# Two up projections by seven half-size products for eight, with the weight sums shared by GpSimd and VectorE

## The reference, cut to what matters

```python
hn = rmsnorm(h, ffn_norm[i])                                   # (512, 1024)
h = h + jnp.square(jax.nn.relu(hn @ ffn_w1[i])) @ ffn_w2[i]    # 1024 -> 4096 -> 1024
gate = jax.nn.sigmoid(rmsnorm(h, ple_norm[i]) @ ple_w_gate[i])
```

## Time and profile before

| | us |
|---|---|
| median of 3 runs | 2130.05 |
| lowest and highest | 2128.93, 2130.39 |
| span of the profiled execution | 2127.2 |
| PE busy in it | 2098.9 |
| DVE, ACT, POOL busy in it | 1014.4, 805.4, 936.1 |

### The profile page before, as it was taken

One profiled execution on the slowest core, in us unless ns is written; L12 is line 12 of the kernel. 1 busy time (PEld: TensorE's weight loads), 2 busy tenths in 40 slices (PEclk: granted clock), 3 DMA queues, 4 the chain that ended last, 5 costly groups with the idle time before them and its releaser, 6 DMA issues.

```text
span 2127.2 us, 26516 instructions
## 1 busy us (share of the span) xinstructions
PE 2098.9 (99%) x9908; PEld 1705.7 (80%) x9908; DVE 1014.4 (48%) x1580; ACT 805.4 (38%) x1243; POOL 936.1 (44%) x436
## 2 busy tenths in 40 slices
PE   9999999999999999999999999999999999999998
PEld 7777888888888866888888887878867888888887
DVE  7996623122356555532132355572454466254463
ACT  7766322122343157322222355352244343232232
POOL 5984544444444410444444442444443444444442
PEclk9999999999999999999999999999999999999999
DMA  5332432222222222232222221222211222322221
GB/s 193 133 115 79 145 113 82 96 100 97 99 81 99 100 90 90 80 117 81 100 97 99 99 91 49 104 82 98 98 60 60 99 90 97 106 84 100 97 99 60
DMA packets 33803, 205.31 MB, mean 97 GB/s; under 512 B 4512, under 2 KB 6688, under 8 KB 10672
## 3 DMA queue, kind: packets, MB, share of 16 engines
q1 hardware_dynamic: 33424, 199.87, 26.6%
q10 hardware_dynamic: 288, 4.19, 0.5%
HBM read 197.73 MB, written 6.32 MB: 96 GB/s over the span
## 4 chain that ended last, share of the span: by engine, by line
PE 60%; issue 23%; POOL 10%; DVE 5%; ACT 1%; DMA 0%; POOLq 0%; SPq 0%; DVEq 0%; ACTq 0%
PE gp L599 19%; PE gp L600 19%; PE gp L601 18%; POOL w_lo L493 9%; DVE ms L1554 3%; POOL pool_sum L516 1%; DMA h<-x_hbm 0%; PE gp L646 0%; PE gp L645 0%; PE gp L647 0%; PE ms L742 0%; PE ms L737 0%; PE gp L945 0%; PE gp L885 0%; DVE acc_sq L1551 0%
## 5 line engine op out<-in xcount | busy, mean ns | idle before, releaser
L493 POOL TENSOR_TENSOR w_lo<-raw,w_hi 128x1024 fp32r<-128x1024 f32 x350 | 848.0, 2426 | 1099.2 <-ACT w_hi L1071 1077.5
L599 PE MATMUL gp<-a_hi,w_hi 128*128 128x512 f32 (+1 forms) x1456 | 567.4, 390 | 1.8 <-DVE a_lo L1554 0.9
L601 PE MATMUL gp<-a_hi,w_lo 128*128 128x512 f32 (+1 forms) x1456 | 563.2, 387 | 0.0
L600 PE MATMUL gp<-a_lo,w_hi 128*128 128x512 f32 (+1 forms) x1456 | 563.1, 387 | 0.0
L1071 ACT ACTIVATE w_hi<-raw 128x1024 fp32r<-128x1024 f32 x349 | 365.5, 1051 | 505.9 <-PE gp L601 434.2
L600 PE MATMUL gp<-b_lo,w_hi 128*128 128x512 f32 (+1 forms) x1216 | 469.7, 386 | 0.0
L599 PE MATMUL gp<-b_hi,w_hi 128*128 128x512 f32 x1184 | 462.8, 391 | 0.0
L601 PE MATMUL gp<-b_hi,w_lo 128*128 128x512 f32 x1184 | 460.6, 389 | 0.0
L599 PEld LDWEIGHTS gp<-a_hi,w_hi 128*128 128x128 f32 x1456 | 273.5, 188 | 60.3 <-POOL w_lo L493 1.5
L600 PEld LDWEIGHTS gp<-a_lo,w_hi 128*128 128x128 f32 x1456 | 273.5, 188 | 56.5 <-issue 1.4
L601 PEld LDWEIGHTS gp<-a_hi,w_lo 128*128 128x128 f32 x1456 | 273.4, 188 | 55.5
(11 more groups left out here) (333 smaller groups left out, 1829.0 us busy)
## 6 DMA issues: line engine op xcount, KB each, us to landing
raw<-w_hbm SPq DMA_DIRECT2D x176, 1024.0 KB, 4.8
proj_scratch<-kT ACTq DMA_DIRECT2D x2, 2048.0 KB, 6.7
fbias<-negc_scratch SPq DMA_DIRECT2D x16, 256.0 KB, 3.4
h<-x_hbm SPq DMA_DIRECT2D x4, 512.0 KB, 7.5
u_pad<-proj_scratch SPq DMA_DIRECT2D x1, 2048.0 KB, 10.1
big<-proj_scratch SPq DMA_DIRECT2D x1, 2048.0 KB, 8.7
out_hbm<-h SPq DMA_DIRECT2D x8, 256.0 KB, 2.2
mem_raw<-mem_hbm SPq DMA_DIRECT2D x1, 1024.0 KB, 12.5
```

The source lines that it names most:

```text
L493: g.tensor_tensor(at(w_lo), src, f32(at(w_hi)), ALU.subtract).then_inc(w_lo_done, 1)
L599: pe.matmul(o, wh, xh, start=start, stop=False)
L600: pe.matmul(o, wh, xl, start=False, stop=False)
L601: return pe.matmul(o, wl, xh, start=False, stop=stop)
```

## The change

The up projection of 512 hidden features (four halves before) becomes one unit. Its weights are seen as four corners: features 0 to 511 or 512 to 1023 (`k`), and two rows of 256 hidden features (`row`). The tokens are halved as well (`HS` = 256). Seven products of corner-size operands, or sums of them, take the place of eight (Strassen's scheme). Each is a slab of the ring: three are corners of the raw weights, four are sums in a new buffer `mix`. Each of the seven is done for two hidden blocks (g = 0, 1) with 4 x 3 matmuls of 256 columns. The partial results stay in the same four banks: `gp` for unit 0 of a chunk, `ms` for unit 1; where a bank's state is needed before more is added, ACT takes a copy (`snap`).

- The four sums of unit 0's weights are made on POOL between its low parts (`mixing_slabs`), those of unit 1 on DVE, ahead of unit 0's row operations.
- The moving operands that are sums (`x_diff`, `xq_hi`, `xq_lo`) are made once a layer, in `mixed_prep` on DVE and `add_and_mix` on ACT.
- Of the hidden result DVE adds up two states, scales them in SBUF and squares; the second row comes out with its sign turned, so that min stands for max. The hidden blocks come in the order `HIDDEN`, and the first down product takes them in that order.
- SP waits, for a slab behind a unit, for the sums too. Both raw slabs of a unit must have come before its first high part.
- The loops over chunks are written out. The projection is loaded back behind the last unit, into `big1` in both layers.

The core of the diff:

```diff
+        for u in range(n):
+            slab_of.extend([(a, (0, 0)), (None, 0), (a, (1, 0)), (a, (1, 1)), (None, 1), (None, 2), (None, 3)])
+            freed_at.extend(Mul(2 * MIX * (at["unit"] + u) + 2 * (j + 1)) for j in range(MIX))
...
+        def mix_steps(at, u, eng, mixed_by):
+            a, n = at["raw"] + 2 * u, at["unit"] + u
+            base = 4 * (n // 2)
+            a11, a12, a21, a22 = corner(0, 0), corner(1, 0), corner(0, 1), corner(1, 1)
+            terms = ((a21, a22), (by_corner(mix[:, 0]), a11), (a12, by_corner(mix[:, 1])), (a21, a11))
+            def step(i):
+                if i == 0:
+                    for b in (a, a + 1):
+                        eng.wait_ge(raw_ready[b % 2], 16 * (b // 2 + 1))
+                if i in (1, 2):
+                    eng.wait_ge(mixed_by, base + i)
+                if n:
+                    eng.wait_ge(w_lo_done, unit_slab[n - 1] + (1, 4, 5, 6)[i] + 1)
+                eng.tensor_tensor(by_corner(mix[:, i]), terms[i][0], terms[i][1], ALU.add).then_inc(mixed_by, 1)
+            return step
...
+                    q.wait_ge(w_lo_done, Pos(slab_done[pos.const - 2], 2 * pos.step, pos.i).at())
+                    if pos.const - 2 in mixed_from:
+                        mixed_by, base = mix_of(mixed_from[pos.const - 2])
+                        q.wait_ge(mixed_by, base + 4)
...
+            def mixing_slabs(l, a):
+                for up in ffn[l]["up"]:
+                    slabs(a, up["slab"] + 1)
+                    step = mix_steps(up, 0, g, mix_pool)
+                    step(0)
+                    step(1)
+                    slab(Pos(up["slab"] + 1))
+                    step(2)
+                    slab(Pos(up["slab"] + 2))
+                    step(3)
+                    slab(Pos(up["slab"] + 3))
+                    a = up["slab"] + 4
+                return a
...
+            def mixed_up(at, u, X, src=None):
+                for j in range(MIX):
+                    pe.wait_ge(w_lo_done, at["slab"] + MIX * u + j + 1)
+                    for g in range(2):
+                        if j < 2 and not u:
+                            free_bank(Pos(at["blk"]), 2 * g + j)
+                        if j >= 4:
+                            pe.wait_ge(snapped, 6 * n + 2 * (j - 4) + g + 1)
+                        for k in range(4):
+                            pe.matmul(o, wh, xh, start=j < 2 and k == 0, stop=False, skip_group_check=True)
+                            pe.matmul(o, wh, xl, start=False, stop=False, skip_group_check=True)
+                            m = pe.matmul(o, wl, xh, start=False, stop=j in (2, 3, 5, 6) and k == 3, skip_group_check=True)
+                        m.then_inc(mul_done, 1)
+                    if first and j == 1:
+                        stat(at, src["acc"] + 7)
...
+            def mixed_unit(at, u, H_, src=None):
+                next_mixed(0)
+                if u:
+                    up_hi(at, H_, 2)
+                    up_hi(at, H_, 3)
+                next_mixed(1)
+                next_mixed(2)
+                snap(T[:, 0], 0, 2, 0)
+                next_mixed(3)
+                snap(T[:, 1], 1, 2, 0)
+                snap(pair_sum[:, 0], 0, 3, 1)
+                next_mixed(4)
+                snap(pair_sum[:, 1], 1, 3, 1)
+                snap(sqb[:, 0, 0:HS], 0, 4, 0)
+                next_mixed(5)
+                snap(sqb[:, 1, 0:HS], 1, 4, 0)
+                next_mixed(6)
+                up_hi(at, H_, 4 * u)
+                up_hi(at, H_, 4 * u + 1)
...
+            def mixed_rows(at, u, H_):
+                if u == 0:
+                    step = mix_steps(at, 1, v, mix_dve)
+                    for i in range(4):
+                        step(i)
+                for row in range(2):
+                    for g in range(2):
+                        if row == 0:
+                            tt(t[:, 0:HS], t[:, 0:HS], t[:, HS:], ALU.add).then_inc(half_row, 1)
+                            tt(t[:, HS:], bank[:, 2 * g + 1, HS:], sqb[:, g, 0:HS], ALU.add).then_inc(rows_out, 1)
+                        tt(t, t, rstd[:], ALU.mult).then_inc(up_scaled, 1)
+                        stt(U[:, k % 2], t, 0.0, t, (ALU.max, ALU.min)[row], ALU.mult).then_inc(full, 1)
+                        if k >= 1:
+                            low_mixed(at, H_, k - 1)
```

More of the change, by code:

```diff
@@ L189, in build @@
     NS = led.count["slab"]
[L190 removed]
+    NRAW = led.count["raw"]
+    assert sorted(slab_at) == list(range(NRAW))
+    slab_done = [0] * NRAW
+    for n, (a, _) in enumerate(slab_of):
+        if a is not None:
+            slab_done[a] = n + 1
+        if a in mixed_from:
+            slab_done[a + 1] = n + 1
     with ExitStack() as ctx:
```

347 lines of the change are left out of this document (241 added, 106 removed).

## The result

The changed kernel takes **2329.01 us** (median of 4 runs, 2327.76 to 2330.87) against 2129.49 us of the kernel before beside it: ratio **1.0938**, 95% interval 1.0922 to 1.0953. It is 200 us slower. The forecast was 2340 us, 2240 to 2405. The profiled execution has a span of 2327.7 us and a mean granted clock of 0.956 (before: 2127.2 us and 0.997).

What follows compares the result with a forecast made beforehand. TensorE's stream was taken to bound the kernel before. Span 2127.2 + 174 (middle chunks) + 28 (first chunks) + 8 (clock) = 2337 us; the runs' median lies 2.9 above the span, so 2340 us, range 2240 to 2405.

Steps and rivals of the forecast that it cites:

- last low part of the hidden operand: Middle chunk, start of down: low part 7 ready at about 70 us, delaying the first down slab by 12.5 us.
- Step 1: Middle chunk: unit 0's second raw slab lands at -13.2 us; POOL's eight operations in a row then end at 7.2.
- The mechanism: Feed-forward layers: two-SBUF-input DVE operations and POOL operations exclude each other and take turns, one each; middle chunk +21.8 us.
- One sign that was named: Named as showing the forecast right: DVE's scalings and squares would have a mean near 1.5 us.
- The stalls: PE's waits in a middle chunk: 1.2, 6.7 and 4.6 us in the units, 12.5 at the start of down.
- a dip of 2 to 3.4 us: Cost of one clock fall behind a stall, mostly hidden by another stall: +8 us in all, bounds 0 and 54.
- Rival C: Clock falls for most of the feed-forward layers, four stalls a chunk near each other: 2390 to 2440 us; chance 13%.
- First chunks: First chunk of each layer: preparation's DVE operations wait for POOL; two PE waits of together 12 to 14 us; both layers +28.
- Eight middle chunks: Each chunk ends at 108.8 us against 87.05 before: +21.8 us, times 8 = +174 us.
- The saving of the products: 256-column products every 0.120 us: a unit takes 20.16 us instead of 21.76, 25.6 us saved over 16 units without waits.
- Rival B: TensorE stays the bound, the lead of three slabs covering delays: 2104 us, up to 2125 with small waits; chance 4%.
- Rival A: No turns in the new phases; row operations fall between POOL's, leaving snapshot waits and down's tail: 2148 us; chance 8%.

Runs made afterwards that it cites:

- no_read: Changed kernel with POOL's low parts and weight sums in the feed-forward layers replaced by fills of about the same length that read nothing: 2170.0 us, ratio 1.0191.
- apart: pool_sums with the row sums, factor, squares and hidden low parts reading one operand from PSUM, as in squares_psum_il: 2273.1 us, ratio 1.0680.
- pool_sums: Changed kernel with all eight weight sums of a chunk on POOL, none on DVE: 2350.0 us, ratio 1.1044.
- warm_tail: As warm, without the 12 added zero-weight products ahead of unit 1's fifth product: 2330.8 us, ratio 1.0949, clock 0.978.
- floor: Changed kernel with weight sums and POOL's weight low parts cut to 8 columns, except in each layer's first chunk (low parts) or first unit (sums): 2183.3 us, ratio 1.0252.
- rows_psum: Changed kernel with the row sum kept in PSUM, so scaling and square read one PSUM operand each; half sum moved later: 2318.4 us, ratio 1.0888.
- best: rows_psum with DVE's four weight sums placed one behind each row block of unit 0: 2303.1 us, ratio 1.0828.
- warm: Changed kernel with 95 zero-weight products a chunk added on PE at its waits in unit 1 and the first down slab: 2328.7 us, ratio 1.0938, clock 0.979.
- squares_psum_il: best with the squares left in PSUM too, for the hidden low parts and ACT's copy to read: 2275.6 us, ratio 1.0685.

## Why the prediction was right

The steps of the forecast for a middle chunk, beside the rows of the third chunk (t = 0 at 467.06):

| step | forecast | measured |
|---|---|---|
| both raw slabs of unit 1 there | 15.4 | 14.7 |
| DVE's sums end | 27.5 | 25.9 |
| second square | 32.3 | 30.4 |
| low part for the fourth product | 36.7 | 34.5 |
| PE's stall for it | 6.7 | 5.3 |
| fifth product starts | 44.2 | 41.9 |
| PE's stall for it | 4.6 | 1.8 |
| the units end (down starts) | 52.8 | 50.5 |
| last low part of the hidden operand | 70 | 66.2 |
| chunk | 108.8 | 107.8 |

Step 1 of the forecast has a slip in its sum, of no weight for the rest: -21.8, 3.5 and 4.8 make -13.5, not -13.2.

**The mechanism** was right: no_read, which takes POOL's reads away and little else, takes away 159 of 200 us; apart against pool_sums, which moves DVE's operands and what hangs on them, gives 77. One sign that was named did not come: squares have a mean of 1.46 us, but scalings 0.86, not near 1.5.

**The sizes.** The stalls were smaller than forecast (15.8 us instead of 25 in this chunk: 0.3 for a snapshot, 5.3, 1.8, and 8.5 at the start of down) and the clock fell for longer: it stood at half for about 20 us of this chunk (30.5 x 0.11 x 2 + 25.5 x 0.27 x 2 from the windows), 190 us more in the whole program than before. I had reckoned with a dip of 2 to 3.4 us, mostly hidden in front of a stall, and put 8 us in the sum, 1 us a chunk; here what this chunk loses beyond its stalls is 8.5 us (107.8 less 15.8 of stalls and 83.5 of products at full clock). In unit 1 the two errors have one cause, and so they cancel: at half clock PE arrives later and waits less, as warm_tail shows. At the start of down only a part cancels: this chunk lost 13.8 us there (57.3 from the first down product to the next chunk, less 43.5), for 12.5 forecast as a stall, but it was 8.5 us of stalls and 5.3 of clock, and the 2 to 3 us behind the last low part have no stall to hide in. That the term came out so close is in part luck. Rival C, with 2390 us or more, is refuted by the time itself; that the clock's falls cost nothing is not shown.

**First chunks.** Forecast +14 us each beyond a middle one; measured 126.3 and 124.8 against 107.9, so +18.4 and +16.9. PE's stalls in layer 0's first chunk:

```profile
241.13 0.58 PE L959 MATMUL gp<-a_hi,w_hi 128*128 128x256 f32 x1 [5.31 <-DVE h L1772]
...
249.34 0.58 PE L959 MATMUL gp<-a_hi,w_hi 128*128 128x256 f32 x1 [3.44 <-DVE h L1772]
256.80 2.08 PE L812 MATMUL ms<-acc_sq,inv_d 128*128 128x512 f32 x2 [4.54 <-DVE acc_sq L1769]
```

Three waits of together 13.3 us, where I took two of 12 to 14, and products at half clock between them. In no_read the first chunk of layer 0 is still 14.9 us longer than the next (103.0 and 88.1): most of this term is the preparation's own operations, not turns. The forecast ascribed it to turns. The preparation's `TENSOR_SCALAR`, which has one SBUF operand, is slowed too: 0.35 us at the least, 1.70 at the median. In floor the first chunk is 27 us longer than the next. What it costs beyond a middle chunk depends on how much of it the middle chunk loses anyway.

**The sum.** Eight middle chunks of 107.9 on average: +167 us (forecast 174); two first chunks: +35 (28); together +202, against a span that grew by 200.5.

**The saving of the products** was as the rows said: 0.119 us a product, a unit in 20.0 us instead of 21.76 (floor). Rival B, that TensorE stays the bound, needs POOL and DVE off the path, and floor shows that even then the tail takes 2.8 to 4.3 us, against 3.5 saved.

**Rival A**, no turns, is refuted by the rows above, but it was right in one thing: the median of the 64 squares is 0.693 us. 24 of them and 4 of the 64 scalings took 2.7 to 2.8 us. That those fall where PE's chain is late, because what is late brings POOL's low parts in a bunch, fits the rows at 514 to 522, but was not tried.

**What failed in expectations after the result**: rows_psum (33 us too low), best (13 above its range) and apart (13 above). They took a turn for one operation of POOL at most, and took away turns without asking which operation would take the next one; in best a snapshot's wait came on top. floor (38 above) left out the first chunks. warm and warm_tail (13 and 11 above) left out that the added products would stand behind the last wait themselves. squares_psum_il hit its number, but not by the waits that it named.

No version beat the kernel before. The nearest that computes the reference, apart, is 6.8% slower.

## What to carry to other kernels

Count the operations of GpSimd and the two-SBUF-operand operations of VectorE as one queue: where together they have little slack in front of a deadline of TensorE, work added to either delays both, however idle each looks alone. Where VectorE must run beside GpSimd, leave one of its operands in PSUM, and check every operation of the chain, since one that is left can take the wait of the others. And before a scheme with fewer multiplications is built, set the tail that it adds at each phase's end against the products saved: here 4.3 us against 3.5, and 2.8 where the clock did not fall. What TensorE does behind the last wait of a phase is the place where a fall of the clock costs.

## What the runs showed of the hardware

- A GpSimd instruction that only writes does not hold up a VectorE operation with two SBUF operands: with fills in place of reads, 58 of 88 us of a chunk on POOL, these stayed at 0.692 us. The Trainium skill (SBUF — State Buffer, "SBUF: two separate sides") says that a VectorE operation with two SBUF inputs meets the lock only against a GpSimd operation that reads SBUF; no_read agrees. For an operation with one SBUF operand this does not hold: beside fills the preparation's `TENSOR_SCALAR` took 0.77 and 0.60 us (at 236.02 and 241.89 of no_read), for 0.35 alone.
- The two engines do not always take turns one each. Beside POOL's operations VectorE mostly got in after one (2.7 to 2.8 us for 0.69, 3.3 for 1.22), but a lone half sum of 0.42 us waited through three of them, 6.99 us in apart, 6.76 in pool_sums (at 479.83) and up to 7.5 in rows_psum (at 609.68). What decides between the two was not found: in rows_psum the same instruction got in after the first of three at 507.31 (1.21 us).
- Time at half clock costs nothing where a wait for another engine comes behind it (7.28 and 7.27 us from the fourth to the fifth product, at full and at half clock), and something where none does: 1.4 us between two chunks of floor whose waits in front were the same, 1.70 and 1.69 us. Why the clock fell behind the one and not behind the other these rows do not show.
